# Seven modulation groups computed on VectorE instead of TensorE, with moved positions and split loads downstream

## What is computed

```python
def adaln(c, w_ada, b_ada):
    mod = jax.nn.silu(c) @ w_ada + b_ada
    return jnp.split(mod[:, None, :], 6, axis=-1)
...
sh1, sc1, gt1, sh2, sc2, gt2 = adaln(c, w_ada, b_ada)
a = modulate(h, norm1_g, sh1, sc1)
rq, rk, rv, rg, sq, sk, sv = split_heads(a @ w_in)
...
h = h + gt1 * merge_groups(ro, rg, so, ret_norm_g, w_out)
b = modulate(h, norm2_g, sh2, sc2)
h = h + gt2 * peer_ffn(b)
```

## Time and profile before

| what | value |
|---|---|
| median of 3 runs | 1953.43 us (1948.82 to 1955.31) |
| profiled execution | 1953.24 us, span 1951.4 us |
| TensorE busy | 1819.1 us, 93% of the span |
| VectorE busy | 1372.5 us, 70% |
| ScalarE busy | 861.8 us, 44% |
| GpSimd busy | 563.1 us, 29% |
| mean granted TensorE clock | 0.973 of 2.4 GHz |

### The profile page before, as it was taken

How to read it: one execution, slowest core, us unless ns; L and a number is a source line. 1 busy time by engine, 2 the same in 40 slices (tenths; PEclk the granted TensorE clock), 3 DMA queues, 4 the chain that set the end, 5 groups by cost and what they waited for, 6 DMA issues and landing times.

```text
span 1951.4 us, 30165 instructions
## 1 busy us (share of the span) xinstructions
PE 1819.1 (93%) x11858; PEld 1731.5 (89%) x11858; DVE 1372.5 (70%) x2534; ACT 861.8 (44%) x1170; POOL 563.1 (29%) x442
## 2 busy tenths in 40 slices
PE   7999988897999999999999999998799998999998
PEld 2799976687999899999999999998799898998997
DVE  4533354536439897788988898687588787888887
ACT  1222244412115445555545545454455454555554
POOL 0111100001110434233553334435444443433310
PEclk9999999888999999999999999999899999999999
DMA  7543232021203988899999999999889988998973
GB/s 278 199 169 133 93 130 99 1 82 71 87 23 101 314 295 300 259 322 310 314 375 322 305 302 366 334 351 361 301 340 372 355 340 346 359 384 333 372 285 111
DMA packets 184608, 497.19 MB, mean 255 GB/s; under 512 B 12924, under 2 KB 75992, under 8 KB 172056
## 3 DMA queue, kind: packets, MB, share of 16 engines
q1 hardware_dynamic: 129096, 293.72, 42.0%
q0 software_dynamic: 55376, 201.61, 28.0%
HBM read 443.90 MB, written 51.12 MB: 254 GB/s over the span
## 4 chain that ended last, share of the span: by engine, by line
PE 60%; DVE 20%; DMA 13%; ACT 3%; issue 2%; POOL 1%; SPq 0%; DVEq 0%; ACTq 0%
PE PS L1009 14%; PE PS L561 9%; PE PS L563 9%; PE PS L562 9%; DMA vrw<-in_peer_v_dram 6%; DVE gat L1807 4%; PE PS L960 4%; DMA gat<-in_peer_v_dram,idx 3%; DMA gat<-in_peer_u_dram,idx 3%; PE PS L625 3%; DVE vl L1943 2%; PE PS L934 2%; PE PS L586 1%; DVE acc L1828 1%; ACT vh L1331 1%
## 5 line engine op out<-in xcount | busy, mean ns | idle before, releaser
L1009 PE MATMUL PS<-wh,vh 128*128 128x352 f32 x1024 | 337.8, 330 | 38.0 <-DVE wl L1945 28.7
L1466 POOL DMA_INDIRECT gat<-in_peer_v_dram,idx x192 | 258.4, 1346 | 383.5 <-DVE acc L1828 351.8
L1466 POOL DMA_INDIRECT gat<-in_peer_u_dram,idx x192 | 244.6, 1274 | 405.6 <-DVE a L1807 333.3
L561 PE MATMUL PS<-XH,uth 128*128 128x352 f32 x1024 | 342.3, 334 | 0.0
L1009 PE MATMUL PS<-wl,vh 128*128 128x352 f32 x1024 | 334.3, 326 | 0.0
L1009 PE MATMUL PS<-wh,vl 128*128 128x352 f32 x1024 | 333.0, 325 | 0.0
L562 PE MATMUL PS<-XL,uth 128*128 128x352 f32 x1024 | 331.4, 324 | 0.0
L563 PE MATMUL PS<-XH,utl 128*128 128x352 f32 x1024 | 331.4, 324 | 0.0
L1807 DVE CUSTOM_DVE_ANT_0 gat<-gat,x 128x1024 f32<-128x1024 f32 x192 | 231.8, 1218 | 33.2 <-DMA gat<-in_peer_u_dram,idx 33.1
L1828 DVE SCALAR_TENSOR_TENSOR acc<-gat,a,acc 128x1024 f32<-128x1024 f32 x184 | 234.1, 1279 | 23.2 <-DMA gat<-in_peer_v_dram,idx 21.5
L561 PE MATMUL PS<-XH,whi 128*128 128x272 f32 x784 | 230.6, 294 | 14.9 <-DVE XL L1756 8.2
(11 more groups left out here) (297 smaller groups left out, 3221.5 us busy)
## 6 DMA issues: line engine op xcount, KB each, us to landing
uraw<-in_peer_u_dram SPq DMA_DIRECT2D x128, 512.0 KB, 5.8
vrw<-in_peer_v_dram SPq DMA_DIRECT2D x64, 1024.0 KB, 7.4
acts_dram<-gel SPq DMA_DIRECT2D x128, 176.0 KB, 6.7
gates_dram<-gst SPq DMA_DIRECT2D x22, 1024.0 KB, 10.4
al<-acts_dram SPq DMA_DIRECT2D x16, 1408.0 KB, 10.6
G<-gates_dram SPq DMA_DIRECT2D x16, 1408.0 KB, 14.4
adaw<-in_w_ada_dram SPq DMA_DIRECT2D x8, 2048.0 KB, 8.0
wraw<-in_w_in_dram SPq DMA_DIRECT2D x7, 2048.0 KB, 7.8
```

The costliest lines, as they stand in the source:

```text
L561: mm(out, ah, bh, start=start, stop=False)
L1009: last = mm(PS[:, k, 0:TD], v_, w_[:, j % 2, :], start=(j == 0 and n == 0), stop=(j == NU - 1 and n == 2))
L1466: nc.gpsimd.indirect_dma_start(out=gat[:, n % NGAT, :], out_offset=None, in_=table, in_offset=bass.IndirectOffsetOnAxis(ap=idx[:, k:k + 1] ...
```

## The change

Groups 5 to 11 are summed on VectorE: for each of the two rows of c, the eight row chunks of `adaw` are multiplied by the matching column of silu(c) (one number per partition) and added up in `adas`, 128 x 512. TensorE then sums over the partitions by eight products of a 128 x 128 piece of `adas` with one column of ones, which gives the columns at once. ScalarE's casts, VectorE's subtractions, the split products and the copy of the result go for these groups, with the operand `silu4` that was made at the start. The sums stand behind the low part of chunks 3 (row chunks 0 to 2 of the next group), 0 (3 to 5) and 1 (6, 7). The load of `adaw` waits for the sums of the group before. Positions in the up-projection move, and the loads of `al` and `G` are made in halves at other positions.

```diff
-EXP_AT = (2, 11, 24, 60, 100)
-SEL_AT = (0, 0, 32, 70, 109)
-GATE_AT = (0, 0, 34, 71, 110)
+EXP_AT = (2, 12, 25, 59, 98)
+SEL_AT = (0, 0, 31, 68, 106)
+GATE_AT = (0, 0, 33, 70, 107)
-GELU_AT = 105
+GELU_AT = 104
-EARLY = 24
+EARLY = 20
-ACT_LOADS = (100, 104)
-V_LOADS = (114, 118)
+ACT_LOADS = (100, 103, 106, 109)
+V_LOADS = (112, 115)
+GATE_LOADS = (NU - 6, NU - 4)
...
-                sp.wait_ge(*((s_ada_mm, 5) if isinstance(g, int) and g == 5 else (s_adau, 4 * (g - 5))))
+                sp.wait_ge(*((s_ada_mm, 5) if isinstance(g, int) and g == 5 else (s_adas, 16 * (g - 5))))
...
-            if j % JB == 1 and 2 <= j // JB + 1 < NU // JB:
-                act_load(j // JB + 1)
-                gate_load(j // JB + 1)
+            if 2 <= j // JB + 1 < NU // JB:
+                if j % JB in (1, 3):
+                    gate_load(j // JB + 1, j % JB // 2)
+                if j % JB in (4, 5):
+                    act_load(j // JB + 1, j % JB - 4)
...
-        def ada_split(g, par, u):
-
-            pe.wait_ge(s_adal, 4 * (g - 5) + u + 1)
-            if u == 0:
-                pe.wait_ge(s_adar, g - 1)
-            for k in (2 * u, 2 * u + 1):
-                w4 = silu4[:, 4 * k:4 * k + P]
-                mm(PS[:, 4 + par, :], w4, adah[:, u % 2, k % 2, :], start=(k == 0), stop=False)
-                last = mm(PS[:, 4 + par, :], w4, adal[:, k, :], start=False, stop=(k == KD - 1))
-            last.then_inc(s_adau, 1)
+        def ada_columns(g, par, col):
+
+            pe.wait_ge(s_adas, 16 * (g - 4))
+            for x in range(4):
+                for t in range(2):
+                    last = mm(PS[:, 7, bass.ds(col + 2 * x + t, 1)], adas[:, par, t, x * P:(x + 1) * P], ones[:, 0:1],
+                              start=True, stop=True)
+            last.then_inc(s_adat, 1)
...
                     if st is gemms[0] and cc == 1:
-                        ada_turn(g + 4, slot, 7, 8 * g)
-                    if st is gemms[0] and cc >= 2:
-                        for u in (2 * cc - 4, 2 * cc - 3):
-                            ada_split(g + 5, 1 - slot, u)
+                        ada_columns(g + 4, slot, 8 * g)
...
+        def ada_sum(g, par, ks):
+
+            for k in ks:
+                if k == 0:
+                    dve.wait_ge(s_adaw, 16 * (g - 3))
+                    dve.wait_ge(s_adat, g - 1)
+                for t in range(2):
+                    a, w, c = adas[:, par, t, :], adaw[:, k, :], siluT[:, k, t:t + 1]
+                    if k == 0:
+                        ts(a, w, c, None, ALU.mult).then_inc(s_adas, 1)
+                    else:
+                        dve.wait_ge(s_adas, 16 * (g - 5) + 2 * k + t - 1)
+                        stt(a, w, c, a, ALU.mult, ALU.add).then_inc(s_adas, 1)
...
-                if st is gemms[0] and cc == 0 and (not isinstance(g, int) or g >= 1):
-                    ada_lo(g + 4, (2, 3))
+                if st is gemms[0] and cc < 2 and (not isinstance(g, int) or g >= 1):
+                    ada_sum(g + 4, slot, ((3, 4, 5), (6, 7))[cc])
                 if st is gemms[0] and cc == 3:
-                    ada_lo(g + 5, (0, 1))
+                    ada_sum(g + 5, 1 - slot, (0, 1, 2))
...
             if st is gemms[0]:
-                ada_lo(st.groups + 4, (2, 3))
+                ada_sum(st.groups + 4, 1, (3, 4, 5, 6, 7))
```

More of the change, by code:

```diff
@@ L165, in build @@
     adaw = at("adaw", RT, [KD, 512])
-    adal = at("adal", RT, [KD, 512], F32R)
     adar = at("adar", RT + 16384, [2, 512])
-    adah = at("adah", RT + 20992, [2, 2, 512], F32R)
-    silu4 = at("silu4", RT + 29184, [4 * KD + P], F32R)
+    adas = at("adas", RT + 20992, [2, 2, 512])
     sel4 = at("sel4", RT + 29184 + 640, [2])
@@ L315, in build @@
     s_xT, s_hT = sem("s_xT"), sem("s_hT")
-    s_s4, s_adah, s_adal, s_adau = sem("s_s4"), sem("s_adah"), sem("s_adal"), sem("s_adau")
+    s_adas = sem("s_adas")
     s_sum = sem("s_sum")
@@ L491, in v_load, with act_load @@
             sp.dma_start(vrw[:, b % 2], v_d[:, 2 * b:2 * b + 2, :]).then_inc(s_v[b % 2], 16)
-        def act_load(c):
+        def act_load(c, h):
             if c < 2:
@@ L499, in act_load, with gate_load @@
                 sp.wait_ge(s_ao[slot], 16 * (JB // 2) * (c + 1))
-            sp.dma_start(al[:, c % 2].rearrange("p j t -> p (j t)"), acts[:, c * JB * TD:(c + 1) * JB * TD]
+            m, n = c * JB + h * JB // 2, JB // 2
+            sp.dma_start(al[:, c % 2, h * n:(h + 1) * n].rearrange("p j t -> p (j t)"), acts[:, m * TD:(m + n) * TD]
                          ).then_inc(s_al[c % 2], 16)
-        def gate_load(c):
+        def gate_load(c, h):
             if c >= 2:
@@ L510, in gate_load @@
                 sp.wait_ge(s_up, NU)
-            sp.dma_start(G[c % 2][:], gates_d[:, c]).then_inc(s_g[c % 2], 16)
+            cols = slice(h * TD // 2, (h + 1) * TD // 2)
+            sp.dma_start(G[c % 2][:, cols], gates_d[:, c, cols]).then_inc(s_g[c % 2], 16)
         sp.wait_ge(gemms[2].lo, 16)
@@ L526, in _ @@
             if m in ACT_LOADS:
-                act_load(ACT_LOADS.index(m))
+                act_load(ACT_LOADS.index(m) // 2, ACT_LOADS.index(m) % 2)
             if m in V_LOADS:
                 v_load(V_LOADS.index(m))
-            if m == NU - 4:
-                gate_load(0)
+            if m in GATE_LOADS:
+                gate_load(0, GATE_LOADS.index(m))
         assert stored == NBLK
@@ L534, in _ @@
         act_store(NU - 1)
-        gate_load(1)
+        gate_load(1, 0)
+        gate_load(1, 1)
         for j in range(NU):
@@ L587, in ada, with ada_turn @@
             last.then_inc(s_ada_mm, 1)
-        def ada_split(g, par, u):
-            pe.wait_ge(s_adal, 4 * (g - 5) + u + 1)
-            if u == 0:
-                pe.wait_ge(s_adar, g - 1)
-            for k in (2 * u, 2 * u + 1):
-                w4 = silu4[:, 4 * k:4 * k + P]
-                mm(PS[:, 4 + par, :], w4, adah[:, u % 2, k % 2, :], start=(k == 0), stop=False)
-                last = mm(PS[:, 4 + par, :], w4, adal[:, k, :], start=False, stop=(k == KD - 1))
-            last.then_inc(s_adau, 1)
-        def ada_turn(g, par, bank, col, n=4):
+        def ada_turn(g, par, bank, col):
             pe.wait_ge(s_adar, g + 1)
             for x in range(4):
-                last = mm(PS[:, bank, bass.ds(col + 2 * x, 2)], adar[0:n, par, x * P:(x + 1) * P], sel4[0:n, :],
+                last = mm(PS[:, bank, bass.ds(col + 2 * x, 2)], adar[0:2, par, x * P:(x + 1) * P], sel4[0:2, :],
                           start=True, stop=True)
+            last.then_inc(s_adat, 1)
[5 more added lines that the diff above has]
+                              start=True, stop=True)
             last.then_inc(s_adat, 1)
@@ L725, in _ @@
             if g >= 1:
-                ada_turn(g - 1, (g - 1) % 2, 6, 8 * (g - 1), 2)
-        ada_turn(3, 1, 6, 24, 2)
+                ada_turn(g - 1, (g - 1) % 2, 6, 8 * (g - 1))
+        ada_turn(3, 1, 6, 24)
         pe.wait_ge(s_adaw, 16)
         ada(4, 0, adaw)
-        pe.wait_ge(s_s4, 1)
         pe.wait_ge(norms[0].sd, 1)
         gemm_start(gemms[0], chunk_by_chunk(norms[0].lo, 0, lambda k: k + 1))
-        ada_turn(4, 0, 7, 0, 2)
+        ada_turn(4, 0, 7, 0)
         gemm(gemms[0])
-        ada_turn(11, 1, 7, 56)
+        ada_columns(11, 1, 56)
         pe.wait_ge(gemms[0].ev, CREDIT + NIN)
@@ L1085, in ada_row @@
         def ada_row(g, par):
-            n = 2 if isinstance(g, int) and g < 5 else 4
-            act.wait_ge(*((s_ada_mm, g + 1) if n == 2 else (s_adau, 4 * (g - 4))))
-            if not isinstance(g, int) or g >= 2:
+            act.wait_ge(s_ada_mm, g + 1)
+            if g >= 2:
                 act.wait_ge(s_adat, g - 1)
[L1091 to L1099, removed]
+            act_(adar[0:2, par, :], PS[0:2, 4 + par, :], ACT.Copy).then_inc(s_adar, 1)
         def scores_out(i, q):
@@ L1114, in group @@
                     c = 4 * g + cc
-                    if st is gemms[0] and cc >= 2:
-                        for u in (2 * cc - 4, 2 * cc - 3):
-                            ada_hi(g + 5, u)
                     act.wait_ge(st.mm, c + 1 + CREDIT)
@@ L1120, in group @@
                          ACT.Copy).then_inc(st.ev, 1)
-                    if st is gemms[0] and cc == 3:
-                        ada_row(g + 5, 1 - slot)
             if st is gemms[0]:
@@ L1335, in gate_row @@
             if j % JB == 0:
-                act.wait_ge(s_g[c % 2], 16 * (c // 2) + 16)
+                act.wait_ge(s_g[c % 2], 32 * (c // 2) + 32)
             if j >= 2:
@@ L1568, in add_squares @@
             dve.sem_inc(s_sum, 1)
[L1571 to L1575, removed]
         add_squares(norms[0])
@@ L1933, in weights @@
             if j % JB == 0:
-                dve.wait_ge(s_al[c % 2], 16 * (c // 2) + 16)
+                dve.wait_ge(s_al[c % 2], 32 * (c // 2) + 32)
             if j >= 2:
```

## The result

The changed kernel takes 1884.44 us (median of 4 runs, 1877.84 to 1886.79), the kernel before 1951.12 us (median of 4). The ratio is 0.966, 95% interval 0.9615 to 0.9705: 66 us faster. The forecast was 1897 us with a range of 1880 to 1921, so the time lies inside it, on the fast side. The profiled execution of the changed kernel is its fastest, 1877.84 us with a span of 1876.1; it is 6.6 us under the median, and the last table of this part shows where about half of that is.

What follows compares the result with a forecast made beforehand. TensorE alone was taken to bound the input projection, while transfers and late loads made it wait in the handover and down-projection. Terms -19.8 - 2 - 13 - 21 = -56 us on 1953.2 gave 1897 us, range 1880 to 1921.

Steps and rivals of the forecast that it cites:

- Part 1: Input projection on TensorE: split products out, one-column products in; -19.8 us, -21 by the lower end, -7 by the upper.
- Part 2: Sums on VectorE in the projection: hidden within 3.8 us of low-part slack; 0 us, up to +7.
- Part 3: Moved positions in the up-projection: fewer waits for exponentials, a new wait at the second choice; -2 us, between -7 and +8.
- Part 4: Handover to the down-projection: gates end 15.5 us earlier, 20 early additions instead of 24; -13 us, ends -20 and 0.
- I give back 3 us for pace: Handover: fewer gathers but three more u rows in the transfers cost 3 of the 15.5 us gained.
- Part 5: Down-projection: al and G in spread halves remove most of TensorE's 28.7 us of waits; -21 us, between -8 and -28.
- The sum of bytes ahead of one v load: Down-projection: bytes queued ahead make v late; with halves at most 3.6 MB in 7.9 us, 1 us over, against 4.5.
- a: Down-projection: halves delay three v loads instead of one, +57 us against the forecast, 1975 us; chance 3%.
- b: Down-projection keeps its waits because the bytes are the same; -35 us in all, 1918 us; chance 10%.
- c: Handover gain eaten by transfers, plus new up-projection waits (+8); 1920 to 1941 us; chance 10%.
- d: Projection doesn't hide its sums: row chunks land 6 us late in seven groups, +42, 1939 us; chance 3%.

Runs made afterwards that it cites:

- d1: Changed kernel with all 16 sums of a group in one piece behind one low part, plus six extra VectorE products; 1928.57 us, ratio 0.9852.
- s2: Changed kernel with first G halves behind the last u row, gate stores halved, early additions paced two per up-projection row; 1874.76 us, ratio 0.9615.
- m1: Kernel before with only the new VectorE sums and column products, everything else as it was; 1937.07 us, ratio 0.9896.
- m2: Kernel before with only the al and G loads halved and spread over the block of eight; 1919.49 us, ratio 0.9813.
- m3: Kernel before with only the changed kernel's up-projection positions (EXP_AT, SEL_AT, GATE_AT, GELU_AT); 1949.07 us, ratio 0.9953.
- e24: Changed kernel with 24 early additions again instead of 20, nothing else undone; 1883.79 us, ratio 0.9622.
- n2: Changed kernel with all four al and G halves issued at row 1 of a block; 1954.04 us, ratio 0.9992.
- n1: Changed kernel with whole al and G loads kept apart, G at row 1 and al at row 4; 1882.26 us, ratio 0.961.
- n3: Changed kernel with whole al and G loads, both at row 1 of a block; 1923.59 us, ratio 0.9867.
- s1: Changed kernel with first G halves behind the last u row and each store of gates in two halves; 1876.61 us, ratio 0.9625.

## Why the prediction was right, and where it was not

The parts measured alone, 20, 9 and 37 us (each known to 5 to 8 us), add up to 66, the whole gain. The forecast had 20, 15 and 21. That the time is inside the range is in part luck: the terms 1 and 5 lie beyond their own ends (-22.4 us against -21, -35 against -28), and part 4 fell short by 6.

**Part 1, right in mechanism, a little too small.** I had -19.8 us. From the first product of the projection to the end of the last columns it is 22.4 us less: 272.03 - 65.3 before (the earlier trace rows has the turn's 270.97 and 1.06), 249.16 - 64.8 after; the table's distance ends at the last product and has 20.5 of them. The columns cost less than any bound of mine: 0.105 us for a record, 1.68 for a group, where I took 1.96 and a lower end of 0.111 a record. Seven groups are 2.0 us of the 2.6 by which the term was too small. The mechanism (split products out, one-column products in, TensorE full throughout) is that of the earlier trace rows.

**Part 2, right.** No wait for a low part or a row chunk in the projection; sums 0.67 us apart; eight loads of adaw in 7.7 to 14.5 us. d1 shows that the cover is real and where it ends; what the piece beyond it costs I had as one for one, and it was 1.6 for one, for the clock.

**Part 3, right in sign, the size uncertain.** -2 us forecast. The u rows to the last gate are 732 us in the mean of eleven kernels with the new positions, 752 in the three with the old. Of these 20 us, 15.5 are the three rows by which the gates end earlier (three places of 5.16); some 5 are a gain. With a spread of 10 us among kernels with equal positions this is no more than a sign. The new wait at the second choice is 2.2 us in the changed kernel and 5.5 at most (in s2); I had 5.

**Part 4, too large.** "I give back 3 us for pace" is the failed term. The gates end 15.5 us earlier, and the handover grows from 51 us (mean of before, m1 and m2) to 59, so 8 us are given back and -7 remain instead of -13; m3, with the positions alone, has 59.7 there. I looked at VectorE and its 39 us of additions; it was done 15 us early and e24 shows that its number didn't matter. What is late is u: three rows more go through while the transfers are full (1.04 and 1.03 in the windows above), and the wait on u rows grew to 11.5 us. With the projection's part the first down product still comes 40.0 us earlier (at 1352.54 and not at 1392.51), where I had said some 35. In these two executions 15.3 us of it lie between the first u row and the first down product; I had 15 for parts 3 and 4 together, one too small and the other too large.

**Part 5, too small.** "Most of the 28.7 us goes: -21 us, between -8 and -28" is the step that failed; it was 35 us in the stage, above my upper end. The waits did go, 24.9 us of them. The missing 10 are the clock, and the row was in my hand: 0.98 over 532 us is 0.02 x 532 = 10.6 us of work lost (8 to 13, as the clock is read to two digits). In windows of the kernel before:

```profile
1550.00:1560.00 10.00, 5.59 (x26) 5.43 (x25) 6.49 (x8) 4.38 (x6) 2.12 (x2) 0.83 0.79 307
1570.00:1580.00 10.00, 10.00 (x65) 10.00 (x64) 9.45 (x12) 5.24 (x8) 5.38 (x4) 1.00 1.00 417
1620.00:1630.00 10.00, 5.89 (x23) 5.69 (x22) 6.49 (x8) 4.37 (x6) 2.38 (x2) 0.66 0.76 298
```

In the window without a wait 65 products are recorded; in the two with one, 26 and 23, fewer than the idle time alone takes away. I counted this in part 4 and left it out here. Waits plus work lost to the clock is an upper estimate, as the clock is also low while TensorE waits: n2 against the changed kernel has 48.7 us more of waits and 0.05 x 567 = 28 us for the clock, 77 in all, and its stage is 71.0 us longer. The Trainium skill, TensorE: Matmul & The Clock Gate, section HAM oscillation - how this bites in real kernels, describes a kernel in which waits for transfers throw the clock back and the products behind them run at half rate; the traces of n2 and the kernel before agree, with 0.95 and 0.98 in the stages that wait for v, and d1's 0.92 shows the same behind waits for VectorE.

The sum of bytes ahead of one v load was the right idea about the places. About the size it was wrong: by it 1.4 MB at one place (n1) should have kept part of the waits, and n1 has 1.7 us of them; and it gives n2 and n3 the same. The Trainium skill, DMA: Bandwidth & Descriptors, section Rules for kernel authors, which stood against the change, is not refuted: whole loads apart are no slower than halves (n1), and at one place halves are 24 us slower than whole ones by the ratios (n2 against n3).

**The rivals.** a (three v loads late instead of one) didn't come in the changed kernel: v loads there land in 4.7 to 11.4 us, median 7.9 (I had said under 10), and TensorE waits 3.8 us on wl. b fell with m2. c holds for its first half: the handover's gain was partly eaten; the new waits were 2 us. d fell: no load of adaw was late enough to be waited for.

## What to carry to other kernels

Price a wait of TensorE with the granted clock of its stage beside it: one minus the clock, times the stage, came on top of the waits here, nearly in full, and both went together. Where a queue carries one urgent stream and some bulk, put the bulk at separate places between the urgent loads first; cutting it into pieces gained nothing here, and pieces left at one place lost 24 us against whole loads there. Work that comes in early at a handover only helps in full if what must pass there after it, here three u rows, finds the transfers free.

## What the hardware showed that I had not expected

- Four transfers of 704 KB in a row cost more than two of 1408 KB: 582.3 against 547.2 us of down-projection, with late v loads of 10.1 to 15.7 us against 10.8 to 13.4.
- A wait of TensorE costs more than its length: 24.9 us of waits made 39.6 us in d1; 48.7 us more of waits in n2 than in the changed kernel made 71.0 us.
- A product of a 128 x 128 float32 operand with a single column takes 0.105 us a record in a row of 16, less than the 0.111 of the 128-column ones in the earlier trace rows.
- An issue on SyncE's queue, 0.33 us at most places, takes 6.83 us behind a store of 1 MB that is 3.4 us old, and 3.81 us in s1, where the store ahead of it is a half.
